# One compare-and-multiply per token for the gate-scaled one-hots, on VectorE instead of a wide compare and six ScalarE scalings

## The reference

```python
# per token: 8 heads, 16 picks each of 128 x 128 experts; i = a * 128 + b for the two key indices
s = einsum('thpd,hpnd->thpn', q, keys);  ts, ti = top_k(s, 16)
best_s, pos = top_k(all sums of two halves, 16);  idx = picked a * 128 + b
gate = softmax(best_s)
hu  = einsum('chkd,cd->chk', u[idx], x)          # 128 picked rows of u per token
act = gelu(hu) * gate
out = einsum('chk,chkd->cd', act, v[idx])        # 128 picked rows of v per token
```

## Time and profile before

| what | value |
|---|---|
| three timed runs | 1715.29, 1722.30, 1724.46 us |
| profiled execution, span (the only time that the profile gives for it) | 1721.0 us |
| VectorE, low halves L1556 | 256 x 1.225 us |
| VectorE, gathered rows L1721 | 192 x 1.220 us |
| VectorE, one-hots L1820 | 128 x 0.95 us |
| ScalarE, high halves L1090 | 256 x 1.057 us |
| ScalarE, copies of a gate batch L1266 | 64 x 2.067 us |
| GpSimd, gather issues L1328 (u) | 192 x 1.459 us |

### The profile page before, as it was taken

One profiled execution on the slowest core, in us unless ns is written; L12 is line 12 of the kernel. 1 busy time (PEld: TensorE's weight loads), 2 busy tenths in 40 slices (PEclk: granted clock), 3 DMA queues, 4 the chain that ended last, 5 costly groups with the idle time before them and its releaser, 6 DMA issues.

```text
span 1721.0 us, 22970 instructions
## 1 busy us (share of the span) xinstructions
PE 1635.2 (95%) x8269; PEld 1397.5 (81%) x8269; DVE 1443.3 (84%) x2707; ACT 781.9 (45%) x1310; POOL 566.3 (33%) x414
## 2 busy tenths in 40 slices
PE   8999899999999999999998999998999999999998
PEld 6876555667999999999998999997778777777787
DVE  4488887866877899989989999838989898899897
ACT  4222223321244444448988999843333333333332
POOL 0000000000003344444555555604445554555450
PEclk9999999999999999999999999999999999999999
DMA  6114122234436899998999999999999999999995
GB/s 218 50 49 41 25 74 86 62 127 131 147 117 240 317 318 343 338 314 277 399 377 344 392 381 394 372 343 380 402 402 395 404 403 385 404 401 399 403 389 171
DMA packets 155351, 482.37 MB, mean 280 GB/s; under 512 B 26031, under 2 KB 43119, under 8 KB 153063
## 3 DMA queue, kind: packets, MB, share of 16 engines
q1 hardware_dynamic: 99943, 279.57, 45.6%
q0 software_dynamic: 55296, 201.35, 31.1%
HBM read 426.17 MB, written 54.42 MB: 279 GB/s over the span
## 4 chain that ended last, share of the span: by engine, by line
PE 59%; DVE 19%; DMA 14%; ACT 4%; issue 3%; SPq 1%; DVEq 0%; POOL 0%; ACTq 0%; POOLq 0%
PE ps L824 18%; PE ps L968 16%; DMA raw<-in_v 10%; PE ps L567 6%; PE ps L778 5%; DVE lo L1556 4%; PE ps L583 4%; PE ps L944 4%; DMA gelu_matrix<-gest 3%; DVE ring L1721 3%; ACT hi L1090 2%; DVE caccb L1424 1%; DVE acc L1725 1%; PE ps L595 1%; PE ps L667 1%
## 5 line engine op out<-in xcount | busy, mean ns | idle before, releaser
L1090 ACT ACTIVATE hi<-raw 128x1024 fp32r<-128x1024 f32 x256 | 270.7, 1057 | 352.2 <-PE ps L968 195.2
L1556 DVE TENSOR_TENSOR lo<-raw,hi 128x1024 fp32r<-128x1024 f32 x256 | 313.5, 1225 | 131.7 <-ACT hi L1090 123.8
L1328 POOL DMA_INDIRECT ring<-in_u,idx x192 | 280.0, 1459 | 423.4 <-DVE hu L1721 261.8
L1328 POOL DMA_INDIRECT ring<-in_v,idx x192 | 273.6, 1425 | 301.7 <-DVE acc L1725 286.0
L824 PE MATMUL ps<-xh,hi 128*128 128x384 f32 x1024 | 351.2, 343 | 12.3 <-DVE lo L1556 11.9
L824 PE MATMUL ps<-xl,hi 128*128 128x384 f32 x1024 | 343.7, 336 | 0.0
L824 PE MATMUL ps<-xh,lo 128*128 128x384 f32 x1024 | 343.6, 336 | 0.0
L968 PE MATMUL ps<-hi,ah 128*128 128x512 f32 x768 | 240.8, 395 | 20.4 <-DVE al L1853 13.8
L1725 DVE SCALAR_TENSOR_TENSOR acc<-ring,hu,acc 128x1024 f32<-128x1024 f32 x192 | 245.5, 1279 | 0.1
L968 PE MATMUL ps<-lo,ah 128*128 128x512 f32 x768 | 238.1, 391 | 0.0
L968 PE MATMUL ps<-hi,al 128*128 128x512 f32 x768 | 237.5, 390 | 0.0
(11 more groups left out here) (223 smaller groups left out, 1953.8 us busy)
## 6 DMA issues: line engine op xcount, KB each, us to landing
raw<-in_uT SPq DMA_DIRECT2D x128, 512.0 KB
raw<-in_v SPq DMA_DIRECT2D x128, 512.0 KB
wring<-in_wblk SPq DMA_DIRECT2D x58, 512.0 KB, 3.5
gelu_matrix<-gest SPq DMA_DIRECT2D x64, 384.0 KB
gate_matrix<-Gs SPq DMA_DIRECT2D x16, 1536.0 KB
gel<-gelu_matrix SPq DMA_DIRECT2D x64, 384.0 KB
Gl<-gate_matrix SPq DMA_DIRECT2D x64, 384.0 KB
wring<-in_wblk SPq DMA_DIRECT2D x16, 256.0 KB, 2.5
```

Source lines behind the costliest of these rows:

```text
L1090: nc.scalar.activation(hi[:, s % 2, :], raw[:, s % RAWS, :], ACT.Copy).then_inc(s_hi, 1)
L1328: pool.indirect_dma_start(ring[:, r % SLOTS, :], None, table, bass.IndirectOffsetOnAxis(idx[:, t, c:c + 1], 0)).then_inc(g_in[r % SLOTS], 16)
L1556: nc.vector.tensor_tensor(lo[:, s % 2, :], raw[:, s % RAWS, :], hi[:, s % 2, :].bitcast(F32), ALU.subtract).then_inc(s_lo, 1)
```

## The change

A is written once, with the gate in it. For each token VectorE issues one tensor-scalar instruction over 128 keys, which compares `iota` with the first index (a per-partition scalar) and multiplies by the gate (another). B stays one wide compare and now stands first. ScalarE's six scalings and their semaphore are gone; TensorE waits for one semaphore, counted once a batch.

```diff
-        s_ab = sem("onehots_ready")
-        s_ag = sem("gates_applied")
+        s_ab = sem("gated_onehots_ready")
...
             for b in range(NBAT):
-                pe.wait_ge(s_ab, 2 * b + 2)
-                pe.wait_ge(s_ag, b + 1)
+                pe.wait_ge(s_ab, b + 1)
                 if b >= ABUF:
                     pe.wait_ge(s_gev, b - ABUF + 1)
...
-            def apply_gates(b):
-
-                act.wait_ge(s_ab, 2 * b + 1)
-                for t in range(BATCH):
-                    tok = b * BATCH + t
-                    ins = nc.scalar.activation(A[:, b % ABUF, t, :], A[:, b % ABUF, t, :], ACT.Copy,
-                                               scale=kT3[:, 2, tok:tok + 1])
-                ins.then_inc(s_ag, 1)
-
             step(U_GATE)
-            apply_gates(0)
             step(U_GATE + 1)
             for b in range(NBAT):
                 i = b // (TBLK // BATCH)
                 o = b % (TBLK // BATCH) * BATCH
-                if b + 1 < NBAT:
-                    apply_gates(b + 1)
                 act.wait_ge(s_gmm, b + 1)
...
                 tok = b * BATCH
-                for dst, half in ((A, 0), (B, 1)):
-                    nc.vector.tensor_tensor(dst[:, b % ABUF], iota.unsqueeze(1).broadcast_to([P, BATCH, NKEY]),
-                                            kT3[:, half, tok:tok + BATCH].unsqueeze(2).broadcast_to([P, BATCH, NKEY]),
-                                            ALU.is_equal).then_inc(s_ab, 1)
+                nc.vector.tensor_tensor(B[:, b % ABUF], iota.unsqueeze(1).broadcast_to([P, BATCH, NKEY]),
+                                        kT3[:, 1, tok:tok + BATCH].unsqueeze(2).broadcast_to([P, BATCH, NKEY]),
+                                        ALU.is_equal)
+                for t in range(BATCH):
+                    ins = nc.vector.tensor_scalar(A[:, b % ABUF, t, :], iota, kT3[:, 0, tok + t:tok + t + 1],
+                                                  kT3[:, 2, tok + t:tok + t + 1], ALU.is_equal, ALU.mult)
+                ins.then_inc(s_ab, 1)
```

## The result

The changed kernel takes 1730.9 us (median of 12 runs, 1727.8 to 1735.8) against 1721.8 us (median of 12 runs, 1715.3 to 1728.7). The ratio is 1.0055 with an interval of 1.0041 to 1.0068: slower by 9 us, where 22 were forecast. The profiled execution has a span of 1728.8 us.

A forecast was written before the change was run, and what follows sets the result against it. In the gate stage TensorE runs back to back and VectorE has only 0.33 of 5.50 us free, so added work makes VectorE the bound. 21.8 + 2 + 0.7 - 2.0 = +22.5 us on 1721.0: forecast 1744 us, range 1722 to 1763.

The forecast's parts named there:

- the pair rows: Group-b convolution's multiply-and-add pairs of the same shape, starting 0.25 to 0.26 us apart; source of 0.26 us an instruction.
- the lower bound of 0.15: Least time for a new VectorE instruction, from a four-element tensor-scalar plus time for 128 elements: 0.15 us.
- gather issues beside the six: Gate stage: GpSimd's gather issues reach into VectorE's six new instructions, 0.1 us a batch, 6.4 us in 64 batches.
- stalls kept: Disturbed gate-stage stretches, where Gelu stores land late: of 5.2 us possible if stalls are not absorbed, 2 kept.
- VectorE's free time that covers it: Gate stage: VectorE's idle time, 30.3 us by busy time, absorbs part of the added work.
- TensorE's one wait for scalings: At the gate stage's start TensorE's wait on the removed semaphore ended last once; a gain of 2.0 us.
- I take 0.1, nearer the two unstretched rows than the stretched one, 6.4 us in 64 batches: Gather-issue cost on VectorE, chosen between 0 and 0.25 us a batch from tensor-scalars of 0.22, 0.22 and 0.42 us.
- which fits into 48.2: Last of seven gate-stage stretches: VectorE's 38.7 + 5.5 = 44.2 us fits its 48.2 us, so growth is 0.
- so alone they are on no calm cycle's path: ScalarE's six scalings, 1.75 us by starts: ScalarE then still waits for TensorE, so removing them shortens no calm cycle.
- ScalarE was the brake: Rival, chance 0.10: ScalarE's chain delays low halves where stores land late; without scalings -15 us, 1707 us, deciding at 0.145 us.
- Hidden after all: Rival, chance 0.12: VectorE's idle 30.3 us covers all added work up to 0.224 us an instruction; no change, 1722 us.
- The signs on late stores and the DMA share: Signs of being right in the gate stage: ScalarE's waits for late stores mostly go; DMA share falls to about 0.91.

The follow-up runs named there:

- e1_relief_alone: The changed kernel with A as one wide compare again, ScalarE's scalings gone and the gates left out of the result; 1695.6 us, ratio 0.9857.
- e2_cost_alone: The changed kernel with ScalarE's six scalings a batch kept behind the new instructions; 1731.9 us, ratio 1.0062.
- e5_one_scalar: The changed kernel with the gate's multiplication taken out of the six instructions, one scalar and one operation each; 1709.8 us, ratio 0.9928.
- e4_rows_earlier: The changed kernel with 9 of the gate stage's 124 gathered rows moved to the stage before; 1725.5 us, ratio 1.0029.

## Why the prediction was wrong

**Right.** The bound: VectorE sets the changed stage, as forecast. Its free time by starts is 0.8 us of 362. The price of an instruction: 0.26 us from the pair rows, 0.257 measured; the lower bound of 0.15 is out. So is the estimate of 0.13 us from the Trainium skill's page "VectorE: DVE Perf Modes", section "The TRN2 errata". The work added: +44.2 us forecast, 98.8 - 55.6 = 43.2 measured. The last stage stayed, the start moved by +0.7 us as forecast (7.3 to 8.0 us from the first one-hot to the first batch).

**Wrong, in size.** The forecast for the stage was +22.5 us; measured are 9.8 us from first to last batch and 0.7 ahead of it, from the first one-hot to the first batch: 10.5. By the terms of the sum (the prediction's 21.8 us are the first two and what is left, -28.8, for free time):

| term | forecast | measured |
|---|---|---|
| VectorE's added work | 44.2 | 43.2 |
| gather issues beside the six | 6.4 | 0 |
| stalls kept | 2.0 | 0 |
| VectorE's free time that covers it | -28.8 | -33.3 |
| start | +0.7 | +0.7, but within the added work |
| other work that the ends of the stretch take in | 0 | 0.6 |
| TensorE's one wait for scalings | -2.0 | in the line of free time |
| sum | 22.5 | 10.5 |

The 0.6 is a remainder: from the first one-hot to the last batch VectorE is occupied for 43.8 us more, of which 43.2 are one-hots. The step that failed most, with 6.4 of the 12.0 us too many, is "I take 0.1, nearer the two unstretched rows than the stretched one, 6.4 us in 64 batches". In the trace after, 57 of the 384 instructions last over 0.40 us, up to 0.55, so durations are stretched beside gather issues as at 559.90. But the distance from the first of the six to the row behind them is 1.54 to 1.56 us in all 64 batches: the next instruction starts no later. The prediction added up a stretched duration, where starts count. The gather issues themselves grew from 1.50 to 1.63 us in the mean (GpSimd's 185.45 us in 124 and 197.69 in 121, the windows of before and after). But in e1_relief_alone, which has no narrow instruction, they take 1.62 us (201.40 in 124), so it is not shown that the six made them longer. The rule of the Trainium skill ("SBUF — State Buffer", section "Who interferes with whom") is that one of the two fully blocks while the other holds the port. VectorE's starts here do not bear it out: 238 of the 384 instructions ran beside a gather issue, and none was held.

The second is the free time. I took it from busy time, 30.3 us, which counts the last 0.08 us of an instruction ahead of every wait as busy though the next could have started; by starts it is 34.1 us, of which 0.8 are left after the change. And I cut the stage into stretches whose growth could not fall below 0, and wrote of the last, "which fits into 48.2": that left 4.0 us of its free time (48.2 - 44.2) unused. (The other way, 3 of the 64 batches, 2.4 us, are in none of the seven stretches.) But VectorE works ahead of TensorE: its last one-hot was ready 14.1 us before TensorE used it, and 8.4 us after the change. Part of the free time lay in that lead, 6.6 us of it in one wait for a high half (its longest), and added work used it up. The lead is thus no cover beside the 34.1 us but a place where they lie.

The third cost nothing in the sum but hid the best result of this case: "so alone they are on no calm cycle's path", and with it the reading that in the batches without a dense step VectorE is the last to finish. The cycle that the prediction looked at has a dense step. In the seven batches without one the scalings are what TensorE waits for, worth 26 us with what hung on late stores and with the clock. e1_relief_alone shows it, and that the forecast came out anywhere near is owed to the other half of the theory: with VectorE full the relief is void (e2_cost_alone).

**The rivals.** "ScalarE was the brake" was given 0.10 and was right about the kernel before (its -15 us would have been -25), wrong about the change at 0.257 us an instruction. Its threshold of 0.145 us was too low: e5_one_scalar pays at 0.196. Between that run's stage of 331.9 us and the changed kernel's 355.3 an estimate by straight line reaches the old 345.5 at 0.231 us, so the change lost by 0.026 us an instruction. "Hidden after all" had the size nearly: 1.0055 is just past the 0.5% that the prediction took as the least that can be told from no change.

Of the signs named, the starts of 0.26 us, VectorE's share over 97% and the unmoved last stage came true. The cycle lasts 5.84 us and not 5.9 to 6.0, and the stage grew by 9.8 us and not by 20 or more, as the 0.1 us a batch and the free time explain. Stretched instructions, a sign of being wrong, are there and harmless. TensorE's waits are 21.0 us and not over 30. The signs on late stores and the DMA share failed: ScalarE's waits for stores stayed (11.6 us for 12.9) and the share fell only to 0.96. TensorE's wait in front of a batch did go and came back in front of a dense step. The batch at 826.93, without a dense step before it, follows its forerunner at 825.59 after 1.34 us. The first dense step behind it finds its low half ready, the second does not:

```profile
832.44 1.50 PE L942 MATMUL ps<-gB,gA 128*128 128x128 f32 x12
837.70 0.45 PE L823 MATMUL ps<-xh,hi 128*128 128x384 f32 x1 [3.76 <-DVE lo L1542]
...
843.54 1.50 PE L942 MATMUL ps<-gB,gA 128*128 128x128 f32 x12
```

TensorE waits 3.76 us for the low half. Then that dense step runs in part at the lower clock, granted 0.71, and it is 5.84 us to the next batch, where the following dense step needs 4.26:

```profile
837.70:843.50 5.80, 5.80 (x24) 5.80 (x25) 5.80 (x13) 0.00 (x0) 3.35 (x3) 0.71 0.93 302
```

That leaves TensorE behind VectorE: the next dense step's low half has been ready for 1.31 us, the following ones' for 0.98, 0.65 and 0.32. It catches up at 5.51 us a batch until it waits for VectorE again, so the lower clock costs the stage nothing here.

**Open.** Which wait makes the stage ahead of the gate stage longer in e4_rows_earlier, though VectorE is busy there for only 271.5 of 315 us (460 to 775 us of the kernel before), was not looked for. Why gather issues take 1.62 us or more in the changed kernel and in e1_relief_alone, and 1.50 before, is open too.

## What to carry to other kernels

Before taking work off an engine, look at the irregular turns of a loop as well as the regular one, and ask for each operand of the waiting instruction how long it had been ready; a wait's label names what ended last in the trace, not what this instruction needed. A late operand can often be made early by order alone, on the same engine, which beats moving it to an engine that has 0.33 us left in a cycle of 5.51. When an engine becomes the bound, count its work by distances between starts, and subtract all of its free time, also that which lies behind its last piece of work for the engine that waits.

## What the runs showed of the hardware

- A VectorE tensor-scalar of 128 x 128 fp32 from SBUF occupies 0.257 us with two per-partition scalars and two operations, and 0.196 us with one of each; a compare of 768 elements occupies 0.869 us. Six narrow ones cost 1.54 us against 0.87 for the wide one.
- A duration stretched beside a GpSimd gather issue (0.42 to 0.55 us for 0.35, 57 times) does not delay the next instruction's start.
- DMA engines at 0.99 share and 389 GB/s over 770 to 1120 us, around the gate stage of e1_relief_alone, did not hold the stage up, though single stores landed late.
- A dense step behind a wait of TensorE of 2.03 to 3.77 us ran in part at the granted clock of 1.2 GHz in several places (granted 0.76 and 0.71 over the two shown), and took the batches' distance from 5.51 to 7.16 us where no wait was in it.
